# Three common stages and the delta rule's first stage ahead of the gated branch's first four, in each prompt chunk

## What is computed

```python
def _layer(x, state, p):
    f = _swiglu(_rmsnorm(x, p['ffn1_norm_pre']), ...)
    x = x + (0.5 * _rmsnorm(f, p['ffn1_norm_post'])).astype(x.dtype)
    m, new_state = _token_mixer(_rmsnorm(x, p['mix_norm_pre']), *state, p)
    x = x + _rmsnorm(m, p['mix_norm_post']).astype(x.dtype)
    ...
```

```python
# delta rule (gdn), 4 heads of 128, per chunk
dec = _segment_decay(cumsum(gc), causal)
A = where(strict, bc[..., :, None] * (kc @ kc.T) * dec, 0.0)
sol = triangular_solve(eye + A, rhs)
u = sol[..., :DV] - sol[..., DV:] @ S
o = (qc * exp(G)) @ S + ((qc @ kc.T) * dec) @ u
S = exp(G_last) * S + (kc * exp(G_last - G)).T @ u
# gated linear attention (gla), 4 heads: a decay for every key channel
Bc = cumsum(gc); att = sum(qc[:, None] * kc[None] * exp(Bc[:, None] - Bc[None]), axis=-1)
o = (qc * exp(Bc)) @ S + att @ vc
S = exp(B_last) * S + (kc * exp(B_last - Bc)).T @ vc
# Mamba-2 (ssd), 8 heads: as the delta rule with a scalar decay, without the solve
```

## Time and profile before

| | us |
|---|---|
| median of 3 runs | 3678.21 |
| the three runs | 3677.89 to 3678.44 |
| the profiled execution, its own time | 3676.62 |
| its span, from first to last instruction | 3674.7 |
| TensorE busy with matmuls | 3349.8 (91%) |
| TensorE busy with weight loads | 3208.6 (87%) |
| VectorE / ScalarE / GpSimd busy | 1266.4 / 784.1 / 1554.4 |
| mean granted TensorE clock | 0.952 |

### The profile page before, as it was taken

One profiled execution on the slowest core, in us unless ns is written; L12 is line 12 of the kernel. 1 busy time (PEld: TensorE's weight loads), 2 busy tenths in 40 slices (PEclk: granted clock), 3 DMA queues, 4 the chain that ended last, 5 costly groups with the idle time before them and its releaser, 6 DMA issues. The chain is left out here.

```text
span 3674.7 us, 69455 instructions
## 1 busy us (share of the span) xinstructions
PE 3349.8 (91%) x25750; PEld 3208.6 (87%) x25750; DVE 1266.4 (34%) x1911; ACT 784.1 (21%) x1346; POOL 1554.4 (42%) x948
## 2 busy tenths in 40 slices
PE   8999899977779998999899998998877799989997
PEld 7999899866658997999889997998666599979997
DVE  2220175376644213220122202753755432132201
ACT  2110132232342112110021102322223411121100
POOL 4555366400005653555445553663000056535553
PEclk9999999999869999999999999999998699999999
DMA  3222122100122221222132321321001222212321
GB/s 121 88 86 85 54 89 86 49 1 0 64 84 68 88 89 58 86 86 85 49 96 86 90 80 50 94 88 41 1 0 64 84 74 90 86 58 86 91 79 67
DMA packets 77407, 258.87 MB, mean 70 GB/s; under 512 B 8272, under 2 KB 10064, under 8 KB 76496
## 3 DMA queue, kind: packets, MB, share of 16 engines
q1 hardware_dynamic: 76976, 256.43, 22.5%
q10 hardware_dynamic: 288, 0.49, 0.0%
HBM read 242.31 MB, written 14.58 MB: 70 GB/s over the span
## 5 line engine op out<-in xcount | busy, mean ns | idle before, releaser
L421 POOL TENSOR_SCALAR wh<-raw 128x1024 fp32r<-128x1024 f32 (+2 forms) x472 | 495.3, 1049 | 2018.8 <-PE ps L460 1223.3
L423 POOL TENSOR_TENSOR wl<-raw,wh 128x1024 fp32r<-128x1024 f32 (+2 forms) x472 | 1059.2, 2244 | 72.0 <-POOL wh L421 3.6
L456 PE MATMUL ps<-hh,wh 128*128 128x272 f32 x4896 | 1023.7, 290 | 57.7 <-DVE hl L1570 44.2
L460 PE MATMUL ps<-hh,wl 128*128 128x272 f32 x4896 | 1018.5, 290 | 0.0
L458 PE MATMUL ps<-hl,wh 128*128 128x272 f32 x4896 | 1016.8, 289 | 0.0
L456 PEld LDWEIGHTS ps<-hh,wh 128*128 128x128 f32 x4896 | 774.5, 190 | 68.8 <-issue 68.0
L458 PEld LDWEIGHTS ps<-hl,wh 128*128 128x128 f32 x4896 | 776.5, 190 | 0.0
L460 PEld LDWEIGHTS ps<-hh,wl 128*128 128x128 f32 x4896 | 771.6, 190 | 0.0
L1606 DVE TENSOR_TENSOR prod<-sil,ps 128x544 f32<-128x544 f32 x88 | 63.5, 721 | 704.4 <-PE ps L460 704.4
L456 PE MATMUL ps<-ah,wh 128*128 128x272 f32 x1408 | 296.0, 291 | 0.0
L460 PE MATMUL ps<-ah,wl 128*128 128x272 f32 x1408 | 291.2, 288 | 0.0
(11 more groups left out here) (369 smaller groups left out, 3587.5 us busy)
## 6 DMA issues: line engine op xcount, KB each, us to landing
raw<-in_up SPq DMA_DIRECT2D x176, 512.0 KB, 3.6
raw<-in_win SPq DMA_DIRECT2D x80, 512.0 KB, 3.6
raw<-in_merge SPq DMA_DIRECT2D x96, 384.0 KB, 3.0
raw<-in_down SPq DMA_DIRECT2D x64, 512.0 KB, 3.5
raw<-in_down SPq DMA_DIRECT2D x32, 384.0 KB, 3.1
raw<-in_wout SPq DMA_DIRECT2D x16, 512.0 KB, 3.6
states<-in_in_gdn SPq DMA_DIRECT2D x2, 2048.0 KB, 8.0
proj<-in_in_ssd SPq DMA_DIRECT2D x2, 2048.0 KB, 15.2
```

Source lines behind the costliest of these rows:

```text
L421: pool.tensor_scalar(hi, src, 1.0, 1.0, MULT, MULT).then_inc(hi_done, 1)
L423: pool.tensor_tensor(lo, src, hi.bitcast(F32), SUB).then_inc(lo_done, 1)
L456: pe.matmul(out, wh[:, j % SPLIT, k, :], mh_[:, c], start=a, stop=False)
L460: last = pe.matmul(out, wl[:, j % SPLIT, k, :], mh_[:, c], start=False, stop=b)
```

## The change

One string is another; no instruction is added or removed. In the new string all three `c` stages and g1 come ahead of l1 to l4; before, they alternated. From the ninth letter on, which is g2 in both strings, nothing is changed. SAMPLE_ORDER stays.

```diff
-ORDER = "clclcllggllgslggslgsglgslgslgslglglglgggg"
+ORDER = "cccgllllgllgslggslgsglgslgslgslglglglgggg"
```

## The result

| | before | after |
|---|---|---|
| median, us | 3678.32 (4 runs) | 3745.28 (4 runs) |
| the runs | 3677.89 to 3678.64 | 3743.29 to 3746.59 |
| ratio of after to before | | 1.0182, 95% interval 1.0164 to 1.0199 |
| profiled execution, own time / span | 3676.62 / 3674.7 | 3743.29 / 3741.3 |
| mean granted clock | 0.952 | 0.941 |

The kernel became 67 us slower; 3740 was forecast, within 3727 to 3751. Of the 66.6 us by which the span grew, 64.2 lie in the eight prompt chunks.

The account below looks back on a forecast made before the run. A chain across engines through the level factors' end was taken to bound the chunk. Six chunks at 6.57 and two at 7.1 gave 53.6, plus 8.8 for the clock: 3678.2 + 62.4 = 3740.6, rounded to 3740, range 3727 to 3751.

Parts of the forecast that it names:

- What bounds the chunk: Whole chunk: a chain across engines; level factors end at 18.87 us from cc, then g3 starts the solve, running to the end.
- First and second term: Head: g1 done first, L1714 ending at 8.9; l_rc then begins at 8.9 instead of 0.31, 8.64 us later.
- Third term, the hole: Head, ScalarE between its two passes over the levels: the hole shrinks from 2.55 to some 0.5 us, gaining 2.07.
- The net of the order: Level factors' end in each chunk: 8.64 - 2.07 = 6.57 us later.
- The layers' first chunks: Two chunks whose head ran at the lower clock: level factors end at 28.3 instead of 21.17, 7.1 us later.
- Fourth term, the clock: TensorE's head at the lower clock, gate sums and L779: 1.1 us a chunk, 8.8 in all, between 0 and 10.8.
- The remark that the products of k at a lower clock would stay hidden: Head, products of k and transposes: slowing by a clock fall stays hidden up to about 2 us, then costs some tenths.
- A sign of being wrong that came up: Chunk from g3's start: prediction wrong if L1729 to next cc, 47 us before, is more than 1 us shorter.
- TensorE's work as the bound: Whole chunk: TensorE's 52.5 us of work bounds it, so moving rows changes nothing, 3678; 3%.
- The rule of the Trainium skill: Improve the engine with highest occupancy, starting sooner what its gaps wait for; g1's spreads start some 4 us sooner.
- The faster rival: ScalarE between L1285 and L1290: hole closes, gated branch starts less than 2.1 us later; up to 17 faster, 3661; 2%.
- The clock costing more, by lasting into the solve: TensorE's rows in the solve stretched by the lower clock: up to 1.5 us a chunk, 12 us, 3752; 12%.

Follow-up runs that it names:

- e7: Kernel before with g3 and s1 ahead of l5 (level factors), g4 ahead of l6, g5 ahead of l7, on all engines; 3671.3 us (0.9984).
- e3: Changed kernel with l1 put back behind c1 on TensorE and VectorE, ScalarE keeping the changed order; 3717.2 us (1.0111).
- e5: Kernel before with g1 three places earlier on TensorE and ScalarE alone, VectorE's order kept; 3675.4 us (0.9997).
- e10: e5 with the extra TensorE products of e12 and two more behind L786; 3663.6 us (0.9956).
- e12: Kernel before with extra TensorE products, four ahead of the first scores and two ahead of the solve's last product; 3664.3 us (0.9964).
- e11: Changed kernel with extra TensorE products: three behind g1's spreads, two behind L779, five ahead of the first scores, two ahead of L652; 3718.6 us (1.0113).
- e2: Kernel before with g1 alone moved, from behind l4 to behind c3, on all engines; 3701.7 us (1.0067).
- e6: Kernel before with four extra TensorE products in the wait ahead of the first scores; 3680.7 us (1.0015).

## Why the prediction was right, and where it was off

**What bounds the chunk.** Right where it was used: the delay at the end of the level factors, 63.6 us in eight chunks, came out as 64.2 at the chunks' ends. But the prediction gave g3's start as what sets the rest, and e7 shows that this is too narrow. With g3 5.7 us sooner and the factors 5.75 later, the chunk takes 0.2 to 0.7 us more: neither g3 nor the factors alone set what follows. Both stand ahead of the rest on VectorE, and the change delayed both. Whether it is what waits for the factors (the scores) or VectorE's work in all that takes g3's lead away, no run parts.

**First and second term.** Right: L1714 at 7.83 (7.8 forecast), `l_rc` at 8.99 (8.9), a delay of 8.68 (8.64). The steps as the prediction shows them, to a tenth, give 8.6 and, for the third term, 2.0 to 2.1; the second decimals of 8.64 and 2.07 aren't worked out there. e3 took 21.8 of the chunks' 64.2 us back by filling the wait for `br`.

**Third term, the hole.** Right: from the end of the differences to the factors' start VectorE needed 6.1 us before and 4.0 after in the second chunk. e5 and e10 test its mechanism with VectorE's order untouched: 1.3 us of the hole were to close, and the chunk was 1.2 shorter wherever the products of k ran at full clock.

**The net of the order**, 6.57 a chunk, was 6.58 between e12 and e11 with the clock up, and 52.1 over eight chunks. So some 53 us of the 67 are the order.

**The layers' first chunks.** Forecast 7.1 without the fourth term; they grew by 6.9 and by 9.4. The forecast took the sums of squares as cold as before, 3.62 us. In the second they were, and k's scaling (L1705) starts at 8.73 from `cc`. In the first they took 2.53, and it starts at 7.67. The second is also 1.4 us longer behind L1729.

**Fourth term, the clock.** The mechanism was right, and the size was too small, by 1.8 us in the prediction's own division: 64.2 - 53.6 = 10.6, where 8.8 was taken and 10.8 was the upper bound. That it stayed under the bound is in part luck, since a part of it stood in no term. The gate sums were cold in all eight chunks and cost 0.92 in place of 0.8; L779 was at full clock in the second chunk and took up to 0.5 us more in others. What was not in the sum is the clock at the start of a chunk: in two of the six chunks that are not a layer's first it was still down, from the end of the chunk before, and the factors came 1.8 us later again (28.14 against 26.35). The fourth chunk after, TensorE from the end of the third chunk on, where eight rows take 1.9 us and then two of the decay sums 0.77 (0.49 before):

```profile
944.53 1.91 PE L659 MATMUL ps<-g,g 128*128 128x128 f32 x8
946.23 1.34 PE L663 MATMUL ps<-g,g 128*128 128x128 f32 x8
949.58 0.30 PE L553 MATMUL ps<-cst,cc 128*128 128x128 f32 x1 [2.00 <-DVE cc L1690]
950.40 0.77 PE L556 MATMUL ps<-tm,cst 128*128 128x128 f32 x2 [0.52 <-ACT tm L1175]
```

The remark that the products of k at a lower clock would stay hidden was right. They ran at full clock in the second chunk (2.0 us for sixteen records) and cold in the seventh (3.2), with the gate sums cold in both, and the factors ended at 26.35 and 26.33. Likewise 28.14 and 28.13 in the fourth (2.0) and the sixth (3.6). VectorE waited 0.78 us for the transposes behind them, and then 1.33 for ScalarE's second pass, which came later. In e5's order the second pass was done before the transposes, and the same fall cost 1.8 (above).

**A sign of being wrong that came up.** The prediction is wrong, it says, if the stretch from L1729 to the next `cc` is more than 1 us shorter than 47. In the fourth and the sixth chunk, those with the cold start, it was 45.6 and 45.7, and in the third and the eighth 48.3 and 48.2. The sum over eight chunks is 374.3 against 373.8, so the delay of the head is passed on in the sum, but not chunk by chunk.

**The rivals.** TensorE's work as the bound: TensorE's busy time rose by 2.3 us and the chunk by 8, so no. The rule of the Trainium skill (Perfetto Trace Analysis, Identifying the Most-Contended Engine and Optimization Strategy) would have had the change be good; TensorE's spreads of g1 did start 4.2 us sooner (3.66 in place of 7.88 from `cc`), and the chunk grew all the same, so here the measurement goes against it. The faster rival: no, as e2 shows. The clock costing more, by lasting into the solve: not in the sum, as the stretch behind L1729 grew by 0.5 us in eight chunks. What the clock cost, it cost nearly all in the heads.

## What to carry to other kernels

In an order that several in-order engines share, price a move by the waits that the moved rows bring with them on each engine, and by what then stands behind those waits. Rows that depend on nothing new are worth most where another branch waits; here VectorE had waits of 2.3 and 3.6 us, which l1 and l2 filled at no cost. A hole in one engine's list is worth closing only as long as the rows that close it don't wait ahead of the longest chain, and a gain of a microsecond per turn of a loop should be looked at turn by turn, since the TensorE clock can take it back in some of them.

## What the runs showed of the hardware beyond that

- In a loop whose turns end in a wait of TensorE, the clock makes turns of equal work differ by up to 2.7 us (66.7 to 69.5 in e5, the layers' first left out). The kernel before has six like turns of 67.96 to 68.08 us, each with its low stretches at the same places; in all kernels tried but e7, some of these turns had products in their heads at the lower clock that ran at the full one before. Where the sums of squares did, four records took 2.6 to 3.6 us in place of 1.88.
- Extra products in TensorE's waits, which compute nothing, made the kernel 0.36% faster (e12) when they covered both long waits, and 0.15% slower (e6) when they covered one. In both, three turns besides the layers' first had low stretches in their heads that weren't there before; e12 gained more than that at the turns' ends.
- A fall of the clock at the same sixteen records of products cost nothing in one order (the changed kernel, factors' end 26.33 against 26.35 us) and 1.8 us in another (e5, 19.4 against 17.6).
- The parts outside the prompt chunks, where no experiment changed anything, took between 3121 and 3131 us in the profiled executions (3669.2 - 547.7 in e7, 3741.3 - 610.4 in the changed kernel). What sets that spread was not tested, and it limits what a difference of 5 us between two kernels here can say.
